# Hybrid attention and expert layer: tile 0's path to its expert indices moves into the attention, and the remaining output products come before all combining

## What is computed

```
h = LN(x)*(1+sc_a)+sh_a;  proj = h @ w_in
o_na   = neighbourhood attention, 8 heads;  o_diff = differential attention, 4 heads (two maps each)
mix = concat(o_na, o_diff) @ w_out
x = LN(alpha*x + (1+g_a)*mix, ln1);  h = LN(x)*(1+sc_f)+sh_f
per token and each of 8 expert heads:
  s = (h @ w_query) against two tables of 128 keys; top 16 of each, top 16 of the 256 sums -> expert[16], g = softmax
  act = gelu(expert_down[expert] . h);  f += sum_k g_k*act_k * expert_up[expert_k]
x = LN(alpha*x + (1+g_f)*f, ln2)
```

## Time and profile before

| | |
|---|---|
| median of 3 runs | 1809.22 us (1809.19 to 1812.42) |
| the profiled execution | 1809.97 us, span 1808.2 us |
| PE, DVE, ACT, POOL busy | 83%, 63%, 21%, 55% |
| bytes moved | 611.24 MB, mean 338 GB/s |
| attention | from 236 to 346 us |
| first gather, gather 20 | 398.80 us, 439.93 us |
| first and last combining | 450 us, 1793 us |

### The profile page before, as it was taken

The page is one execution under the profiler, slowest core; times in us unless marked ns, Lnnn a source line. Parts: engine busy times, 40 slices in busy tenths (PEclk is TensorE's granted clock), DMA queues, the critical chain, the costliest instruction groups (busy, mean ns, idle before and its releaser), DMA issues.

```text
span 1808.2 us, 14312 instructions
## 1 busy us (share of the span) xinstructions
PE 1497.5 (83%) x4104; PEld 676.3 (37%) x4104; DVE 1141.0 (63%) x2717; ACT 386.2 (21%) x984; POOL 995.0 (55%) x1053
## 2 busy tenths in 40 slices
PE   5899989898689789789778979877798877777776
PEld 4444456556234234234223434322343322222222
DVE  5453057569567787566666766677666766666741
ACT  1111145322121221221211221121121211111220
POOL 2100000015777677677677767777776777777770
PEclk9799999999999999999999999999999999999998
DMA  9678420118999999999999999999999999999992
GB/s 310 240 262 205 121 70 1 70 38 283 407 409 410 407 409 409 407 409 409 407 409 409 409 407 409 409 409 411 409 408 378 392 409 409 410 409 409 409 410 112
DMA packets 194019, 611.24 MB, mean 338 GB/s; under 512 B 31231, under 2 KB 31639, under 8 KB 193783
## 3 DMA queue, kind: packets, MB, share of 16 engines
q0 software_dynamic: 147456, 536.94, 74.9%
q1 hardware_dynamic: 46135, 72.16, 12.3%
q10 hardware_dynamic: 352, 1.25, 0.2%
HBM read 606.92 MB, written 3.34 MB: 338 GB/s over the span
## 4 chain that ended last, share of the span: by engine, by line
DMA 48%; PE 22%; POOL 14%; issue 7%; DVE 6%; ACT 2%; SPq 1%; DVEq 0%; POOLq 0%
DMA big<-in_expert_up,expert_idx 23%; DMA region_v<-in_expert_up,expert_idx 15%; PE pair L599 13%; POOL big L589 10%; DMA big<-in_expert_down,expert_idx 7%; PE pair L791 6%; POOL region_v L589 3%; DMA region_v<-in_expert_down,expert_idx 3%; DMA big<-in_w_ada 1%; ACT big L886 1%; DVE big L1300 1%; PE pair L734 1%; DVE region_v L1300 1%; SPq L447 1%; PE pair L724 1%
## 5 line engine op out<-in xcount | busy, mean ns | idle before, releaser
L791 PE MATMUL pair<-big 128*128 128x512 f32 x1544 | 757.6, 615 | 181.6 <-DMA big<-in_expert_up,expert_idx 161.8
L1300 DVE CUSTOM_DVE_ANT_0 big<-big,pair 128x1024 f32<-128x1024 f32 x378 | 460.9, 1220 | 308.2 <-DMA big<-in_expert_down,expert_idx 307.3
L791 PEld LDWEIGHTS pair<-big 128*128 128x128 f32 x1544 | 265.5, 190 | 602.8 <-issue 541.0
L589 POOL DMA_INDIRECT big<-in_expert_up,expert_idx x386 | 365.8, 948 | 159.1 <-PE pair L791 108.4
L589 POOL DMA_INDIRECT big<-in_expert_down,expert_idx x378 | 358.4, 948 | 130.1 <-issue 112.8
L791 PE MATMUL pair<-region_v,big 128*128 128x512 f32 x504 | 246.8, 614 | 56.0 <-DMA region_v<-in_expert_up,expert_idx 55.8
L599 PE MATMUL pair<-big 128*128 128x512 f32 (+2 forms) x624 | 257.1, 595 | 5.3 <-ACT big L940 3.3
L1300 DVE CUSTOM_DVE_ANT_0 region_v<-region_v,pair 128x1024 f32<-128x1024 f32 x134 | 163.5, 1221 | 94.3 <-DMA region_v<-in_expert_down,expert_idx 92.8
L963 ACT ACTIVATE big<-ident,big 128x128 f32<-128x128 f32 x512 | 156.8, 388 | 204.2 <-DVE big L1249 202.3
L589 POOL DMA_INDIRECT region_v<-in_expert_down,expert_idx x134 | 128.5, 959 | 103.9 <-DVE expert_idx L1238 50.1
L555 POOL TENSOR_SCALAR small<-small 128x4 f32<-128x4 f32 x5 | 1.2, 231 | 314.5 <-DVE small L1178 292.6
(11 more groups left out here) (143 smaller groups left out, 963.5 us busy)
## 6 DMA issues: line engine op xcount, KB each, us to landing
big<-in_w_ada SPq DMA_DIRECT2D x12, 2048.0 KB, 15.4
big<-in_w_query SPq DMA_DIRECT2D x8, 2048.0 KB, 19.0
big<-in_w_in SPq DMA_DIRECT2D x6, 2048.0 KB, 15.7
big<-in_expert_up,expert_idx POOLq DMA_INDIRECT x386, 18.1
big<-in_expert_down,expert_idx POOLq DMA_INDIRECT x378, 18.1
big<-in_w_out SPq DMA_DIRECT2D x2, 2048.0 KB, 10.3
big<-na_scr SPq DMA_DIRECT2D x24, 128.0 KB, 5.9
region_v<-in_expert_down,expert_idx POOLq DMA_INDIRECT x134, 18.1
```

The costliest lines, as they stand in the source:

```text
L589: nc.gpsimd.indirect_dma_start(places[place], None, (expert_down if kind == "down" else expert_up)[0], bass.IndirectOffsetOnAxis(expert_id ...
L791: last = nc.tensor.matmul(pair[t % 2][:, s * HALF:(s + 1) * HALF], diag[:, j, :], places[place][:, s * HALF:(s + 1) * HALF], start=(h == 0 ...
L1300: v.tensor_tensor_reduce(out=places[place], in0=places[place], in1=u_cur[:, :], scale=1.0, scalar=0.0, op0=ALU.mult, op1=ALU.add, accum_ou ...
```

## The change

The tables and buffers around the attention are rewritten. Tile 0's `mix_t` and `out` stand in the attention (after steps 17 and 18), as do its transposes of u (step 28), its first queries (steps 30 to 33) and key scores (34). DVE does tile 0's layer norms behind the scores of heads 19 to 25 and `choose(0, ...)` behind those of heads 36 to 43; the inverse roots of tile 0 come from GpSimd and not from ACT, and the ln1 rows are loaded a second time. u of tile 0 is transposed twice, once for the early queries and once after the attention. After the attention come out(1), u_t(0), the other queries of tile 0, out(2), out(3). Everything for tile 1's queries moves behind slots 0 to 35, three matmuls a slot. `add_mix(1)`, `add_mix(2)` and `add_mix(3)` stand behind dots 7, 11 and 17, and tile 1's `ln_step`s behind dots 8 to 15. Two later query groups go two a slot; the others keep one. `EVAC_AFTER` is 3. `mix_t` has one buffer where it had two; `gate_arg` and the attention's probabilities lie elsewhere. The number of gathers, their order and their places are as before.

```diff
+FIRST_TILE = {17: [("mix_t", (0, 0)), ("mix_t", (0, 1)), ("out", (0, 0))], 18: [("out", (0, 1))],
+              28: [("u_first", (0,)), ("u_first", (1,))],
+              30: [("query", (0, 0, 0, 1))], 31: [("query", (0, 1, 0, 1))], 32: [("query", (0, 2, 0, 1))],
+              33: [("query", (0, 3, 0, 1))], 34: [("key_scores", (0, 0))]}
+LN_FIRST = {19: (0,), 20: (1,), 21: (2,), 22: (3,), 23: (4,), 24: (5,), 25: (6, 7)}
+CHOOSE_FIRST = {36 + i: (2 * i, 2 * i + 1) for i in range(8)}
...
-    g += mix(0) + mix(1) + u_columns(0) + keys_of(0, 0) + mix(2) + keys_of(1, 0) + mix(3)
-    g += u_columns(1) + keys_of(0, 1) + keys_of(1, 1)
+        g += FIRST_TILE.get(a, [])
+    g += [("mix_t", (1, s)) for s in range(2)] + [("out", (1, s)) for s in range(2)]
+    g += [("u_t", (0, s)) for s in range(2)]
+    g += [("query", (1, b, 0, 1)) for b in range(4)] + [("key_scores", (1, 0))]
+    for t in (2, 3):
+        g += [("mix_t", (t, s)) for s in range(2)] + [("out", (t, s)) for s in range(2)]
...
-EVAC_AFTER = 8
-LN_AT = {4: 2, 5: 3}
+SCHEDULE = [(0, 4, [("u_t", (1, s)) for s in range(2)]),
+            (4, 3, [("query", (0, b, 1, 1)) for b in range(4)]), (19, 1, [("key_scores", (0, 1))]),
+            (20, 3, [("query", (1, b, 1, 1)) for b in range(4)]), (35, 1, [("key_scores", (1, 1))]),
+            (36, 2, [("query", (2, b, 0, 2)) for b in range(4)]),
...
+EVAC_AFTER = 3
+LN_AT = {0: 1, 4: 2, 5: 3}
+ADD_AT = {7: ((1, 0), (1, 1)), 11: ((2, 0), (2, 1)), 17: ((3, 0), (3, 1))}
...
+            gate(0)
+            ln_deviation(0)
+            ln_deviation(1)
             for head in range(HEADS):
-                if head > 0:
-                    expert_gelu(head)
-                    if head + 1 < HEADS:
-                        gate(head + 1)
+                expert_gelu(head)
+                if head + 1 < HEADS:
+                    gate(head + 1)
```

More of the change, by code:

```diff
@@ new lines, with ended_at @@
+EVAC_AFTER = 3
+LN_AT = {0: 1, 4: 2, 5: 3}
+ADD_AT = {7: ((1, 0), (1, 1)), 11: ((2, 0), (2, 1)), 17: ((3, 0), (3, 1))}
+RESIDUAL_AFTER = {13: 0, 17: 1, 29: 2}
+STEPS = {}
+for _first, _rate, _groups in SCHEDULE:
+    _steps = [(g, k) for g in _groups for k in (range(KB) if g[0] in ("query", "out") else (None,))]
+    for _n, _step in enumerate(_steps):
+        STEPS.setdefault(_first + _n // _rate, []).append(_step)
+def ended_at(slot):
+    return [g for g, k in STEPS.get(slot, []) if k in (None, KB - 1)]
@@ L160 @@
+GROUPS = FIRST_GROUPS + [g for i in range(SETS) for g in ended_at(i)]
 INDEX = {g: i for i, g in enumerate(GROUPS)}
@@ L195 @@
 GATHERS = gather_order()
-FIRST_SETS = 20
+FIRST_GATHERS = 20
 PLACE_OF, LAST_USE, USES = {}, {}, {}
@@ L780, in _ @@
             pe.wait_ge(act_evac, firsts_act)
-            pe.wait_ge(dve_evac, EVACS_DVE)
+            pe.wait_ge(dve_evac, sum(EVAC[g][0] for g in range(len(FIRST_GROUPS))))
             for at in range(SETS):
@@ L964, in diagonals @@
                                          scale=weights[:, head % 2, j:j + 1]).then_inc(diag_done, 1)
-                    if at >= EVAC_AFTER and group_at(at - EVAC_AFTER):
-                        evacuate(INDEX[group_at(at - EVAC_AFTER)])
+                    for group in ended_at(at - EVAC_AFTER):
+                        if group[0] not in ON_DVE:
+                            evacuate(INDEX[group])
             def deviation(t):
@@ L1007, in ln_step @@
                 x1, tmp = x_sb[:, t, :], ln_tmp[:, 0, :]
+                rows = ln1_first if t == 0 else ln1_rows
+                rstd = ln_rstd if t == 0 else ln_std[:, 1:2]
                 if step in (0, 4):
@@ new lines, in _ @@
+                    finish_maps(v, dve, link, dve_evac, len(ATT) - 1, row_inv, row_sum, exp_done, neg_lambda, ratio, diff_probs, diff_done)
+                if kind == "out" and args[0] == 0:
+                    add_mix(*args)
+                if kind == "scores" and args[1] == maps_of(args[0]) - 1:
+                    for step in LN_FIRST.get(args[0], ()):
+                        ln_step(0, step)
+                    for step in CHOOSE_FIRST.get(args[0], ()):
+                        choose(0, step)
@@ L1307, in _ @@
                         choose(head + 1, 2 * j + 1)
-                    if (head, j) == (0, 10):
-                        add_mix(TILES - 1)
+                    for group in ADD_AT.get(at, ()):
+                        add_mix(*group)
                     if j >= TOPK // 2 and head in LN_AT:
```

362 lines of the change are left out of this document (180 added, 182 removed).

## The result

The changed kernel takes 1823.33 us (median of 4 runs, 1822.36 to 1824.02), the kernel before 1809.2 beside it: ratio 1.0075, 95% interval 1.0062 to 1.0087. The change makes the kernel slower, as predicted, but by 14 us where 5 to 6 were forecast, and 1823.33 lies just outside the range of 1804 to 1822. The profiled execution took 1822.36 us, its span is 1819.6 (before: 1809.97 and 1808.2).

The account below looks back on a forecast made before the run. TensorE bounds the attention part, DMA the part from gather 20 on. 1809.97 + 8.6 (gather 20 later) + 2 - 5.2 + 0.5 = 1815.9 for an execution like the profiled one, so 1815 us; range 1804 to 1822.

Parts of the forecast that it names:

- The attention, 36.8 us longer: Attention: tile 0's steps put into it cost nearly their full length, 15.9 + 6.6 + 9.0 + 5.3 = 36.8 us.
- The norms' stretch: Heads 19 to 26 of the attention: DVE's added add_mix and layer norms make TensorE's transposes 6.6 us later.
- u and the queries: Attention: tile 0's u transposes, four query blocks and key scores, less two absorbed waits, add 9.0 us.
- From head 36 to the end: Late attention: choose(0) on DVE costs 4.3 us and the clock 1 us, together 5.3 us.
- From the attention's end to gather 20, 66.7 us: After the attention: TensorE's chain through the last output product takes 66.7 us; with the longer attention gather 20 goes 8.6 later.
- DVE's long wait for the root behind the copies of mix_t(3): At dot 10, ln_step(1) waits for ACT's root; DVE idles some 19 us, without cost since gather 19 leaves at 58.
- The start from empty and two matmuls a slot, 2 + 0.5 us: Expert stage: DMA starting empty costs about 3.0 + 1.2 us of full rate, net +2; two matmuls a slot +0.5.
- The stall at slot 349, -5.2 us: Expert stage: EVAC_AFTER 3 removes TensorE's wait at slot 349 and regains 5.2 us of DMA.
- Find their copy in a head whose weights are there: New table: key scores at slots 99, 185, 223, 264 and 349 were checked as not waiting on a next-head copy.
- a stall of the new order's own: Rival: new copy order makes a stall, or late combining holds gathers from 36 on; 3 to 8 us more, chance 0.06.
- growths of 30 to 33 us: No-change rival: attention grows 30 to 33 us and two gains pay for it; 1809 to 1812 us, chance 0.26.
- The rule on regimes that want different engines: Skill's rule: interleaving regimes may help, so the change should gain; the prediction kept to 8.6 us later by rows.

Follow-up runs that it names:

- e4: Changed kernel with the 16 steps of choose(0) moved from heads 36 to 43 to right behind the attention; 1833.11 us (one run).
- e3: Changed kernel with the two add_mix of tile 1 behind dot 3 in place of dot 7; 1815.18 us, ratio 1.0028.
- e1: Changed kernel with key scores (2, 1) at slot 66 in place of slot 58; 1818.84 us, ratio 1.0045.
- e5: Changed kernel with key scores (2, 1) at slot 66 and the two add_mix of tile 1 behind dot 3; 1811.57 us, ratio 1.0011.
- e2: Kernel before with only EVAC_AFTER changed, 3 in place of 8; 1809.65 us, ratio 0.9995.
- f10: Changed kernel with key scores (2, 1) at slot 66, tile 1's add_mix behind dot 3, copies from slot 339 on 8 slots behind; 1811.47 us, ratio 1.0008.
- f5: Changed kernel with key scores (2, 1) at slot 66 and tile 1's add_mix behind dot 3, repeated on another chip; 1812.08 us, ratio 1.001.
- e6: Changed kernel with key scores (2, 1) at slot 66, tile 1's add_mix behind dot 3, key-score copies of slots 349 and 350 8 slots behind; 1811.59 us, ratio 1.0007.

## Why the prediction was right and wrong

**The attention, 36.8 us longer: right (35.4).** The same points stand in both timelines: the scores of head 19, the transposes of head 26 (the earlier trace rows before), the scores of head 36; the kernel before, then the changed one:

```profile
275.82 0.76 PE L724 MATMUL pair<-big 64*128 64x192 f32 x4
...
313.07 0.70 PE L724 MATMUL pair<-big 64*128 64x256 f32 x2
```

```profile
291.08 0.76 PE L748 MATMUL pair<-big 64*128 64x192 f32 x4
...
316.66 1.09 PE L759 MATMUL pair<-ident,big 128*128 128x128 f32 x4 [1.04 <-DVE big L1368]
...
343.15 0.70 PE L748 MATMUL pair<-big 64*128 64x256 f32 x2
```

Up to head 19 the changed kernel is 15.3 us late, for tile 0's output product (15.9 charged). The norms' stretch takes 25.6 us where it took 296.10 - 275.82 = 20.3 (the prediction had 20.0): 5.3 in place of 6.6, with TensorE waiting for DVE at its end. From there to head 36, with u and the queries, 26.5 in place of 17.0: 9.5, where 9.0 were charged. From head 36 to the end 37.2 in place of 32.0: 5.3, as charged, of which e4 gives back 4.4 when `choose(0)` is taken away. So the mechanism is right term by term; that the sum is within 1.4 us is helped by one term too long and one too short, and by executions whose attention ends up to 3 us apart.

**From the attention's end to gather 20, 66.7 us: right (66.3),** with its wait of 5.8 for `add_mix(1)` (6.05 in the profile, confirmed by e3's 7.9 us with the slow products). DVE's long wait for the root behind the copies of mix_t(3) is there too (19.3 us, some 19 forecast) and costs nothing, as said: when gather 19 is out, gather 20 waits 7.8 us more for TensorE. Together 6.8 us later, 8.6 forecast; the error is that of the attention.

**The start from empty and two matmuls a slot, 2 + 0.5 us: right.** The stage is 1328.0 us in e1, 1.8 more than before, and 1328.8 in e5. From gather 20 to 470 us the windows of the changed kernel lack 4.4 us (130 GB/s to 450, then 327 and 403), those of the kernel before 1.4 (365 to 450, then 405 and 403); the difference of 3.0, less one gather of 1.28, is 1.7. That leaves next to nothing for two matmuls a slot, which no run tried alone. The 1.2 in the forecast's 3.0 + 1.2 stands in no row that it cites.

**The stall at slot 349, -5.2 us: wrong, this is the step that failed most.** The stall goes, and nothing is gained: the stage without it is the same to 0.1 us in e2, and with it put back in f10 it is 1.1 us shorter than in f5 and 0.4 shorter than in e6, about the scatter. The working took the mean rate over 16 engines for the work lost. The bound that should have stood beside the 5.2 was nothing: the windows say how long fifteen engines had no work, and not whether the last one had.

**"Find their copy in a head whose weights are there": wrong by omission.** I had asked for each key score of the table at which diagonal its copy stands and whether TensorE waits for it. For slot 58 TensorE does not wait, so it is not in the prediction's list. What I had not asked is who stands behind the waiting copy on ACT: two diagonals on, the root for which DVE waits. The chance of 0.06 for a stall of the new order's own held the case that came, at 2.9 us in the stage and 4.5 between the medians (e1), where I had named 3 to 8.

In sum: 6.8 + 1.8 + 2.9 + 0 = 11.5 us against 11.4 of span; forecast were 8.6 + 2 + 0.5 - 5.2 = 5.9. The two errors in the stage, 5.2 and 2.9 us, point the same way; the start, 1.8 us earlier than forecast, hides a part of them, and in this execution it is early: e1, the same up to there, has its gather 20 at 448.78, near the 448.5 of the forecast. The medians differ by 14.1; the time around the span is 1 us longer in this execution (2.8 for 1.8), and the profiled executions lie 0.8 above the one median and 1.0 below the other.

One sum among the rivals was off by a microsecond: growths of 30 to 33 us give 1808 to 1811 by the forecast's own terms, not 1809 to 1812.

**The rule on regimes that want different engines** (the Trainium skill, "Perfetto Trace Analysis", "Optimization Strategy"), weighed in the prediction, is neither borne out nor refuted as a whole: steps of DVE in the attention cost 4.4 us where the same steps behind it cost 12.5 (e4), so interleaving did help there, while the output product of TensorE cost its full length in the attention (15.3 us; from one to the next behind it 15.7, 414.86 to 430.59).

## What to carry to other kernels

For a copy that is drained late, list what stands behind it on the draining engine, not only who waits for the copy: an engine that normally runs ahead is held to the pace of the slowest, and a scalar result that another engine wants soon (a root, a gate) may stand two instructions on. Before a hole in the DMA rate is priced, look at how the traffic ends: if a sixteenth of the rate goes on alone for some us, a stall shorter than that lag may be free (here 5.1 us of it beside a lag near 10), and a delay in front of the full-rate stage counts in full. Where a long stage starts at one event, put everything that this event does not need behind it, and check only that it is done before the next resource runs out.
